# A two-block kernel: expert values weighted earlier among the queries, gate tables read earlier, one-hots on one engine, another order at the end

## The reference, cut to what matters

```
q = (x @ w_query) as 8 heads x 2 halves x 128
s = q . sub_keys                     # 128 scores for each half
sv, si = top_k(s, 16)                # of each half
cand = sv[0][:, None] + sv[1][None]  # 256 candidates
fv, fpos = top_k(cand, 16)           # 16 experts of the 16384
g = softmax(fv)
out = sum over 8 heads x 16 experts of  g * gelu(x . u[e]) * v[e]
x = x + g2 * out; result = rmsnorm(x) * final_g
```

## Time and profile before

| what | us |
|---|---|
| median of 3 runs (2660.41 to 2666.75) | 2660.56 |
| the profiled execution | 2658.6 |
| its span | 2655.9 |
| TensorE busy in the span | 2491.8 |
| VectorE busy | 1485.2 |
| ScalarE busy | 602.3 |
| GpSimd busy | 432.5 |

### The profile page before, as it was taken

How to read it: one execution, slowest core, us unless ns; L and a number is a source line. 1 busy time by engine, 2 the same in 40 slices (tenths; PEclk the granted TensorE clock), 3 DMA queues, 4 the chain that set the end, 5 groups by cost and what they waited for, 6 DMA issues and landing times.

```text
span 2655.9 us, 24709 instructions
## 1 busy us (share of the span) xinstructions
PE 2491.8 (94%) x8808; PEld 1431.0 (54%) x8808; DVE 1485.2 (56%) x3368; ACT 602.3 (23%) x1482; POOL 432.5 (16%) x351
## 2 busy tenths in 40 slices
PE   6999999999999999999998887799999999999997
PEld 3454555444444444444467665666665666656563
DVE  5444454220105424223657799847686877777777
ACT  2022364110000002222422245501111112111111
POOL 0000000000000000000000155523333333333331
PEclk9999999999999999999999998999999999999999
DMA  9531011112127521111032376889999999999996
GB/s 378 230 119 60 36 48 48 64 67 91 63 108 302 196 90 64 63 64 64 16 143 104 112 280 238 300 356 415 412 417 406 417 416 417 414 417 415 416 396 259
DMA packets 120740, 592.31 MB, mean 223 GB/s; under 512 B 10000, under 2 KB 42768, under 8 KB 76592
## 3 DMA queue, kind: packets, MB, share of 16 engines
q0 software_dynamic: 40656, 321.93, 29.9%
q1 hardware_dynamic: 46224, 247.48, 24.1%
q10 hardware_dynamic: 33744, 21.40, 2.7%
HBM read 571.90 MB, written 18.87 MB: 222 GB/s over the span
## 4 chain that ended last, share of the span: by engine, by line
PE 79%; DMA 10%; DVE 8%; ACT 1%; issue 1%; POOL 0%; DVEq 0%; ACTq 0%; POOLq 0%
PE PS L622 25%; PE PS L1591 13%; PE PS L1644 13%; PE PS L652 8%; DMA arena<-in_u_turned 5%; PE PS L1164 4%; DMA arena<-in_peer_uv 4%; PE PS L1210 3%; PE PS L807 2%; PE PS L1552 1%; PE PS L827 1%; PE PS L816 1%; DMA arena<-in_ada 1%; DVE arena L2219 1%; PE PS L1185 1%; PE PS L1614 1%
## 5 line engine op out<-in xcount | busy, mean ns | idle before, releaser
L1591 PE MATMUL PS<-hT,arena 128*128 128x256 f32 x2048 | 479.6, 389 | 32.6 <-DMA arena<-in_u_turned 32.5
L1591 PEld LDWEIGHTS PS<-hT,arena 128*128 128x128 f32 x2048 | 397.7, 195 | 146.8 <-DMA arena<-in_u_turned 55.5
L2351 POOL DMA_INDIRECT arena<-in_peer_uv,arena x163 | 219.3, 1346 | 1000.2 <-DVE arena L2147 470.2
L622 PE MATMUL PS<-arena,ring 128*128 128x512 f32 x832 | 359.2, 593 | 2.1 <-issue 0.8
L622 PE MATMUL PS<-hT,ring 128*128 128x256 f32 (+1 forms) x928 | 302.7, 486 | 2.9 <-ACT hT L442 2.9
L622 PEld LDWEIGHTS PS<-arena,ring 128*128 128x128 f32 x832 | 157.0, 190 | 203.2 <-issue 201.9
L622 PEld LDWEIGHTS PS<-hT,ring 128*128 128x128 f32 x928 | 179.6, 195 | 122.4 <-issue 105.0
L2194 DVE SCALAR_TENSOR_TENSOR arena<-arena 128x1024 f32<-128x1024 f32 x134 | 171.8, 1282 | 129.3 <-ACT arena L1816 129.1
L1644 PE MATMUL PS<-arena,hT 128*128 128x512 f32 x512 | 231.5, 595 | 6.3 <-DMA arena<-in_peer_uv 4.6
L1644 PE MATMUL PS<-arena,ring 128*128 128x512 f32 x512 | 230.1, 593 | 1.4 <-DMA arena<-in_peer_uv 0.8
L2176 DVE CUSTOM_DVE_ANT_0 arena<-arena 128x1024 f32<-128x1024 f32 x163 | 198.3, 1221 | 44.9 <-DMA arena<-in_peer_uv,arena 44.3
(11 more groups left out here) (349 smaller groups left out, 2765.5 us busy)
## 6 DMA issues: line engine op xcount, KB each, us to landing
ring<-in_wstream SPq DMA_DIRECT2D x45, 2048.0 KB, 7.9
arena<-in_u_turned SPq DMA_DIRECT2D x128, 512.0 KB
arena<-in_peer_uv SPq DMA_DIRECT2D x128, 512.0 KB, 14.7
arena<-in_ada POOLq DMA_DIRECT2D x24, 2048.0 KB, 9.7
gate_tables<-arena ACTq DMA_DIRECT2D x16, 1024.0 KB, 5.3
arena<-gate_tables SPq DMA_DIRECT2D x16, 1024.0 KB, 15.7
arena<-in_peer_uv,arena POOLq DMA_INDIRECT x163
xT<-in_xT POOLq DMA_DIRECT2D x1, 2048.0 KB, 18.9
```

The source lines that it names most:

```text
L622: ins = pe.matmul(o, l, r, start=(a == 0), stop=(a == len(lhs) - 1))
L1591: ins = pe.matmul(dense_bank(j), ubuf[j % 3][:, tile(k)], hT[:, k, 256:512], start=(k == 0), stop=(k == KD - 1))
L2351: pool.indirect_dma_start(rows[j], None, ap["peer_uv"], bass.IndirectOffsetOnAxis(ap=eidx[:, t, e:e + 1], axis=0)).then_inc(landed[j], 16)
```

## The change

Seven edits, all in the part after 1355 us:

- `values_after(b)` goes from 11, 14, 16, 19, 21, 24, 26, 29, 31 (beats 0 to 8) to 5, 7, 9, 11, 14, 16, 18, 20, 23, 25, 27, 29 (beats 0 to 11); QBEAT goes from 9 to 12.
- The turn of the second token tile and the gain row move from behind queries 6 and 9 to behind 3 and 5.
- DOT_PAIRS: the eight pairs of dense dots that come before the loop move from beats 11 to 15 and 19 (three) to 12 to 16, 18 and 19 (two).
- `first_one_hots` runs on VectorE for all 64 groups; before, GpSimd made each fourth, between its gathers.
- SyncE issues first-row reads 15 to 18 after the first value and gate reads, not before them.
- At the end of the beats TensorE does beat 19's values before its dots.
- In the last three chunks (LAST) the matmuls of tile 3 come behind all those of tile 2, and tile 2 is finished as soon as its own are done, with its scaling before tile 3's first step.

```
 def values_after(b):
-    return 11 + (5 * b + 1) // 2
+    return 5 + 9 * b // 4
...
-QBEAT = 9
-DOT_PAIRS = {11: 1, 12: 1, 13: 1, 14: 1, 15: 1, 19: 3}
+QBEAT = 12
+LAST = 3
+DOT_PAIRS = {12: 1, 13: 1, 14: 1, 15: 1, 16: 1, 18: 1, 19: 2}
...
-def made_on_pool(g):
-    return g % 4 == 3
...
-            for j in range(AHEAD + 3):
-                if j == 0:
-                    sp.wait_ge(mm_done, MM0["pq"] + 1)
+            def load_first_rows(j):
                 if j >= 3:
                     sp.wait_ge(s_done, j - 2)
                 sp.dma_start(ubuf[j % 3], ap["u_turned"][j]).then_inc(u_loaded[j % 3], 16)
+
+            sp.wait_ge(mm_done, MM0["pq"] + 1)
+            for j in range(2 * DOT_PAIR0[NBEAT - 1] + 3):
+                load_first_rows(j)
...
             load_values(2)
+            for j in range(2 * DOT_PAIR0[NBEAT - 1] + 3, AHEAD + 3):
+                load_first_rows(j)
...
-                if i == 6:
+                if i == 3:
                     pe.wait_ge(tt_ev, 1)
...
-                if i == 9:
+                if i == 5:
                     pe.wait_ge(tt_ev, 2)
...
+            values(beat_picks(NBEAT - 1))
             beat_dots(NBEAT - 1)
-            values(beat_picks(NBEAT - 1))
...
+            def second_rows(c, td):
+                for half in range(2):
+                    ins = pe.matmul(bank(2 + 2 * td + half), weights_of(c)[:, tile(td)], vbuf[c % 3][:, half * 512:half * 512 + 512],
+                                    start=(c == 0), stop=(c == NCHUNK - 1))
+                return ins
...
-                for td in range(2):
-                    for half in range(2):
-                        ins = pe.matmul(bank(2 + 2 * td + half), weights_of(c)[:, tile(td)], vbuf[c % 3][:, half * 512:half * 512 + 512],
-                                        start=(c == 0), stop=(c == NCHUNK - 1))
-                ins.then_inc(d_done, 1)
+                ins = second_rows(c, 0)
+                if c == NCHUNK - 1:
+                    ins.then_inc(d_first, 1)
+                if c < NCHUNK - LAST:
+                    second_rows(c, 1).then_inc(d_done, 1)
...
+            for c in range(NCHUNK - LAST, NCHUNK):
+                second_rows(c, 1).then_inc(d_done, 1)
...
-                    if not made_on_pool(g):
-                        first_one_hots(g)
+                    first_one_hots(g)
...
-            for t, step in ((1, 0), (1, 1), (1, 2), (1, 3), (2, 0), (2, 1), (2, 2), (3, 0), (3, 1), (3, 2), (2, 3), (3, 3)):
+            for t, step in ((1, 0), (1, 1), (1, 2), (1, 3), (2, 0), (2, 1), (2, 2), (2, 3), (3, 0), (3, 1), (3, 2), (3, 3)):
...
-                while made < 16 and PREVIOUS[n] is not None and PREVIOUS[n] >= first_pick(TABLE_BEAT + made // 2):
-                    first_one_hots(4 * made + 3)
-                    made += 1
```

More of the change, by code:

```diff
@@ L1282, in build @@
         picks_ok, picks_pe, picks_ev = sem("dense_picks"), sem("dense_picks_turned"), sem("dense_picks_copied")
-        a_ok, b_ok, gates_ex = sem("first_one_hots_dve"), sem("second_one_hots"), sem("dense_gate_exps")
+        a_ok, b_ok, gates_ex = sem("first_one_hots"), sem("second_one_hots"), sem("dense_gate_exps")
         g_pe, g_ev = sem("gate_tables"), sem("gate_tables_copied")
@@ L1289, in build @@
         s_done, s_ev, w_ok, d_done = sem("dense_dots"), sem("dense_gelu"), sem("dense_weights"), sem("dense_values")
-        a_pool = sem("first_one_hots_pool")
+        d_first = sem("dense_values_first_tile")
         x_copied = sem("x_copied")
@@ L1604, in gate_tables @@
             def gate_tables(g):
[L1606 to L1609, removed]
+                pe.wait_ge(a_ok, g + 1)
                 pe.wait_ge(b_ok, g // 2 + 1)
@@ L1801, in copy_query @@
                     copy_scores(i // 2 - 1)
-                if i in (1, 6):
-                    t = i // 6
+                if i in (1, 3):
+                    t = i // 3
                     act.wait_ge(tt_pe, t + 1)
                     act.activation(h2tok[t].rearrange("p (a n) -> p a n", a=2), PS[:, 6:8, :], ACT.Copy).then_inc(tt_ev, 1)
-                if i == 9:
+                if i == 5:
                     act.wait_ge(g2_pe, 1)
@@ L2238, in last @@
                     else:
-                        dve.wait_ge(d_done, NCHUNK)
+                        if t == NGT:
+                            dve.wait_ge(d_first, 1)
+                        else:
+                            dve.wait_ge(d_done, NCHUNK)
                         own(dve.tensor_tensor(a, PS[:, 2 * t - 2:2 * t, :], g2row[:, :, :], ALU.mult))
```

## The result

The changed kernel takes 2729.85 us (median of 4, 2726.93 to 2730.87) against 2663.29 us for the kernel before in the same session, a ratio of 1.0248 with a 95% interval of 1.023 to 1.0266: 2.5% slower. Its profiled execution has a span of 2724.8 us, 68.9 more than before.

| segment (marks from the timelines of VectorE and TensorE) | before | after | change | forecast |
|---|---|---|---|---|
| start to the first job | 1368.6 | 1372.2 | +3.6 | 0 |
| first job to beat 12's job (query stage) | 163.0 | 212.4 | +49.4 | +49.7 |
| beat 12's job to the last one-hot (table stage) | 183.4 | 192.5 | +9.1 | +13.8 |
| last one-hot to the first value matmul of chunk 0 (hand-over) | 33.8 | 40.9 | +7.1 | -7 |
| from there to the start of the last matmul (loop) | 892.9 | 897.1 | +4.2 | 0 |

The account below looks back on a forecast made before the run. TensorE was 94% busy, with the last third held by transfers as much. Terms +49.7 + 3 + 10.8 - 7 - 4.3 = +52.2 us on the profiled 2658.6 gave 2711 us, range 2680 to 2738.

Parts of the forecast that it names:

- the hand-over backfires: Rival, 14%: dot 15 waits behind gates and gathers, hand-over +3 us instead of -7, one-hots +17; 2727 us.
- Step 1, turn-taking: Query stage: needed queries fall behind waits on VectorE's dots, six stalls at beats 3, 4, 6, 7, 10, 11; net +49.7 us.
- Step 2, gathers into the weight ring: Behind the query stage: picks 12 to 14 get slots only after query 31, so VectorE waits for gathers; +3 us.
- Step 3, one-hots: Table stage: 64 more one-hot instructions on VectorE, 17.3 us, less its 6.5 us of waits there; +10.8 us.
- Step 4, the hand-over: Before the loop: early reads and values ahead of dots refill idle transfer time, less dot 15's late start; -7 us.
- named as a sign: Hand-over: if right, the first gate read comes some 6 us after the last table.
- The bookkeeping in idle transfer time: Hand-over: 0.40 x 21.4 = 8.6 us of idle transfer time counted as refilled.
- Step 5, the end: After the loop's last matmuls: tile 2's finish is covered and tile 3 starts sooner; -4.3 us.

Follow-up runs that it names:

- q6: The changed kernel with values_after(b) = 6 + 9b//4, one query later, nothing else; 2687 us.
- q7: The changed kernel with values_after(b) = 7 + 9b//4, two queries later, nothing else; 2669 us, ratio 1.0017.
- only_q: The kernel before with the new values_after, QBEAT 12, earlier token turn and gain row, first five dot pairs a beat later; 2713.2 us, ratio 1.0186.

## Why the prediction was right, point by point

The time was forecast as 2711 us and came out as 2729.85, inside the range of 2680 to 2738, which took in the rival "the hand-over backfires". The mechanism was right for the largest term, and one step was wrong in sign.

*Step 1, turn-taking: right, in place and size.* The query stage grew by 49.4 us for 49.7. Six waits stand at the six beats named, 78.3 us in sum for 79.5; the gather waits are gone; and one query decides, as `q6` and `q7` show. Two sizes are off against each other: the clock cost 1.9 to 2.6 us a turn and not 2.5 throughout, and the first diagonal took 1.3 us longer, because ScalarE loaded a table (1.28 us) only after the dot.

*Step 2, gathers into the weight ring: right.* +2.1 us (the wait of VectorE above; the table stage of `only_q` is 2.1 longer than before) for +3.

*Step 3, one-hots: right in kind, too large.* 7.0 in the changed kernel, 7.6 measured alone, for +10.8. The old blocks' waits went, as I had assumed. The term that was mis-sized is what VectorE's instructions take. I divided the length of eight, 2.14 us; from start to start eight take 2.05, 0.256 each, which is 0.9 us over 64. The larger part I had left out: VectorE's own one-hots became shorter once GpSimd made none beside them. Each stretch counted once, the 192 `first_one_hots` instructions covered 50.8 us before, 0.265 each, and the 256 now cover 65.8; the 32 of `second_one_hots` went from 37.5 to 36.3 us. That is 2.6 us.

*Step 4, the hand-over: wrong in sign.* It grew by 7.1 us, and the loop behind it by 4.2, for -7. The step that failed is "the reads of gates and values start when the last store lands (5.3 us)": it landed after 17.8 us, with the value read issued just ahead of it and the gathers that I had counted as a gain beside it. The first gate read came 19 us after the last table, and not the 6 that I had named as a sign. Dot 15 then waited 13.5 us where I had allowed some 4 for all of it. The bookkeeping in idle transfer time failed as well: the share in the first 32 us of the loop fell from 1.01 to 0.67, which is 10.9 us of transfer time for the 8.6 refilled. The rival "the hand-over backfires" (14%) had the late rows, and a price 10 us above the forecast's; it was 18 with the loop. Its total, 2727 us, is nearly what was measured, but by luck: it held 17 us for step 3, which took 7.

*Step 5, the end: right.* It shrank by 4.5 us for 4.3.

Sum: 52.2 forecast, 68.9 in the profiled executions and 66.6 in the medians. Of the 16.7 missing, 18.3 are the hand-over and loop, 3.6 the first job's spread, less 4.7 in the table stage and 0.5 elsewhere. The direction and most of the size came out right because the largest term was read from an order, which needs no rate to be known.

## What to carry to other kernels

When work is moved up in an in-order queue, list for each consumer which item it needs and whether that item now stands behind a wait on the consumer itself: one place too far and two engines take turns, and the price goes by the number of items concerned (here 56 us for two queries' shift, six turns). Before transfers are moved earlier, ask what small and urgent one, like a store that others wait on or the next operand, will then stand beside or behind them; here that cost more than the idle time refilled. And transfers made before a loop that is bound by transfers are a gain only if others can take their place in it; here the gathers that went early left a hole.

## What the runs showed of the hardware

A 1 MB store of gate tables, which landed in 5.3 us at the median, took 16.8 to 18.0 us in the five kernels where a 512 KB read was issued 1.1 us ahead of it and four 1 MB gathers 0.8 to 6.1 us behind it. With the gathers alone it took 5.7 to 6.1 us, with the read alone 7.7. TensorE returned at half clock (0.50 granted) from idles of 7.9 us and more each time, and from one of 2.96 us, but the values behind idles of 1.3 to 1.5 us took their 1.98 us.
